# One layer of a fused two-block kernel: the 64-step scan with heads on their own partition halves and one triangle of its inverse

## What is computed

```python
    def step(state, inp):
        r_t, k_t, v_t, w_t, kk_t, a_t = inp
        sa = jnp.einsum('bhij,bhj->bhi', state, -kk_t)
        state = (state * w_t[:, :, None, :]
                 + sa[..., None] * (kk_t * a_t)[:, :, None, :]
                 + v_t[..., None] * k_t[:, :, None, :])
        y_t = jnp.einsum('bhij,bhj->bhi', state, r_t)
        return state, y_t
    ...
    _, y = lax.scan(step, state0, (seq_first(r_h), seq_first(k_h), seq_first(v_h),
                                   seq_first(w_h), seq_first(kk_h), seq_first(a_h)))
    y = jnp.moveaxis(y, 0, 1)
    mean = jnp.mean(y, axis=-1, keepdims=True)
    var = jnp.mean(jnp.square(y - mean), axis=-1, keepdims=True)
    y = ((y - mean) * lax.rsqrt(var + GN_EPS)).reshape(B, S, RWKV_CH) * gn_w.astype(F32) + gn_b.astype(F32)
    ...
    y = y + bonus.reshape(B, S, RWKV_CH)
    return (y * g.astype(F32)).astype(p_rwkv.dtype)
```

## Time and profile before

| | us |
|---|---|
| median of three runs (1587.70, 1587.82, 1590.32) | 1587.82 |
| time of the profiled execution | 1589.53 |
| its span, first to last instruction | 1587.7 |
| PE busy in it | 1328.5 |
| DVE busy in it | 1034.8 |

### The profile page before, as it was taken

How to read it: one execution, slowest core, us unless ns; L and a number is a source line. 1 busy time by engine, 2 the same in 40 slices (tenths; PEclk the granted TensorE clock), 3 DMA queues, 4 the chain that set the end, 5 groups by cost and what they waited for, 6 DMA issues and landing times. The chain is left out here.

```text
span 1587.7 us, 18244 instructions
## 1 busy us (share of the span) xinstructions
PE 1328.5 (84%) x6818; PEld 917.9 (58%) x6818; DVE 1034.8 (65%) x2387; ACT 405.7 (26%) x843; POOL 295.3 (19%) x297
## 2 busy tenths in 40 slices
PE   5996788998568888888888877777999788799988
PEld 2974377777533333333333322224899667799978
DVE  1697377775677878787787777655552677455442
ACT  3314300003501111111110101012553444544431
POOL 0003200000054444444344334330000000000000
PEclk9997799899889999999999999999999898899999
DMA  9455821117299999999999999997355006245443
GB/s 399 176 193 231 339 110 73 62 64 308 80 396 421 422 420 421 421 422 421 420 412 415 420 421 407 421 421 300 111 208 209 4 1 266 106 160 194 178 159 133
DMA packets 48184, 426.59 MB, mean 269 GB/s; under 512 B 5344, under 2 KB 5472, under 8 KB 5600
## 3 DMA queue, kind: packets, MB, share of 16 engines
q0 software_dynamic: 36864, 268.45, 40.8%
q1 hardware_dynamic: 11232, 156.98, 25.6%
HBM read 424.36 MB, written 1.05 MB: 268 GB/s over the span
## 5 line engine op out<-in xcount | busy, mean ns | idle before, releaser
L1277 PE MATMUL bank<-arena 128*128 128x512 f32 x1024 | 499.5, 615 | 128.9 <-DVE arena L1420 128.6
L1277 PEld LDWEIGHTS bank<-arena 128*128 128x128 f32 x1024 | 176.5, 190 | 436.9 <-DVE arena L1420 285.3
L1458 DVE CUSTOM_DVE_ANT_0 arena<-arena 128x1024 f32<-128x1024 f32 x256 | 313.6, 1225 | 149.2 <-DMA arena<-experts_in,arena 146.0
L1204 POOL DMA_INDIRECT arena<-experts_in,arena x256 | 274.5, 1072 | 606.0 <-PE bank L1277 352.9
L467 PE MATMUL bank<-rounded,rounded 128*128 128x256 f32 x1144 | 334.9, 293 | 45.7 <-DVE rounded L430 36.0
L469 PE MATMUL bank<-rounded,ring_r 128*128 128x256 f32 x1144 | 328.4, 287 | 0.0
L468 PE MATMUL bank<-rounded,rounded 128*128 128x256 f32 x1144 | 327.2, 286 | 0.0
L444 DVE TENSOR_TENSOR ring_r<-ring,rounded 128x1024 fp32r<-128x1024 f32 (+2 forms) x137 | 171.9, 1268 | 144.1 <-ACT rounded L439 144.1
L467 PEld LDWEIGHTS bank<-rounded,rounded 128*128 128x128 f32 x1144 | 222.5, 194 | 50.4 <-issue 27.6
L468 PEld LDWEIGHTS bank<-rounded,rounded 128*128 128x128 f32 x1144 | 223.7, 196 | 3.0 <-issue 2.9
L469 PEld LDWEIGHTS bank<-rounded,ring_r 128*128 128x128 f32 x1144 | 223.3, 195 | 0.0
(11 more groups left out here) (264 smaller groups left out, 1109.8 us busy)
## 6 DMA issues: line engine op xcount, KB each, us to landing
...
arena<-experts_in,arena POOLq DMA_INDIRECT x256, 13.6
...
```

The source lines that it names most:

```text
L1204: pool.indirect_dma_start(rows[:, r % GRING, :], None, experts_in, bass.IndirectOffsetOnAxis(ap=expert[:, tt, at:at + 1], axis=0)).then_in ...
L1277: ins = pe.matmul(psum[2 * tt + half][:, :], diag[:, r % DIAGS, :], rows[:, r % GRING, D + 512 * half:D + 512 * half + 512], start=(h == 0 ...
L1458: dve.tensor_tensor_reduce(rows[:, r % GRING, 0:D], rows[:, r % GRING, 0:D], utok[:, tt, :], 1.0, 0.0, ALU.mult, ALU.add, hdot[:, r:r + 1] ...
```

## The change

**Operands.** The block-diagonal operands and all their memsets and copies are gone, in the preparation and in the scan. Each head's product is a matmul of its own of 64 by 64 on its own partitions (`product`, two for each tile, first head 0, then head 1, into the same bank at partitions 0 to 63 and 64 to 127).

**Steps.** A step covers all four tiles in one bank. Only one triangle of the inverse is kept (R, with the powers P and M). The inverse of the whole triangle isn't made: V1 applies the diagonal part's inverse to the values, and H1, H2, H3 apply x = V1 - S x three times. There are 12 steps of `INVERSE`, which don't need the state, and 7 of `STATE`.

**Order.** `ORDER` runs the inverses of chunks 0 and 1 side by side, then the state steps of chunk 0 between the inverse steps of chunk 2, those of chunk 1 between those of chunk 3, and then the state steps of chunks 2 and 3 alone. Rows 13 to 17 and their columns are put between steps. ACT copies the results of eight of the steps, DVE the rest. The statistics of each chunk are taken one part at a time behind later steps, and the root of the variance by two functions, Ln and Exp, once for each chunk (`roots_of`). The scaling and the bias of the normalization are folded into `gate` and `bv`.

```diff
         B0 = 8960
-        BDk, BDb, BDc, BDr, BDv = (area(B0 + i * 2048, CT, NC, 2, C) for i in range(5))
-        RH = area(B0 + 10240, CT, NC, 2, C)
...
-                for b in (BDk, BDb, BDc, BDr, BDv):
-                    g(pool.memset(b[0:64, :, :, 1, :], 0.0))
-                    g(pool.memset(b[64:128, :, :, 0, :], 0.0))
                 pool.memset(dec[:, :, :, 0:1], 1.0).then_inc(rw["zero"], 1)
-                pool.wait_ge(rw["xs"], NPROJ)
-                for hh in range(2):
-                    s = slice(64 * hh, 64 * hh + 64)
-                    g(pool.tensor_copy(BDv[s, :, :, hh, :], by_chunk(xs[s, 8:12, :])))
 
             @block.vector
...
-                v(dve.tensor_tensor(T0, T0, T3, ALU.mult))
-                for hh in range(2):
-                    s = slice(64 * hh, 64 * hh + 64)
-                    dve.tensor_copy(BDk[s, :, :, hh, :], by_chunk(T0[s]))
...
-                act.wait_ge(rw["kap"], CT)
-                act.wait_ge(rw["rs"], CT)
-                act.wait_ge(rw["bs"], 1)
-                for hh in range(2):
-                    s = slice(64 * hh, 64 * hh + 64)
-                    act.copy(BDc[s, :, :, hh, :], RH[s, :, :, 0, :])
-                    act.copy(BDr[s, :, :, hh, :], RH[s, :, :, 1, :])
-                    act.copy(BDb[s, :, :, hh, :], bS[s])
                 for q in (9, 10, 11):
                     act_mod_row(act, q)
...
+        INVERSE = ("G1", "G3", "G2", "PM2", "TVB", "L1R", "PM4", "TK", "L2R", "M8", "L3R", "SM")
+        STATE = ("RN", "V1", "H1", "H2", "H3", "ST", "Y")
+        ORDER = [(k, c) for k in INVERSE for c in (0, 1)]
+        for c in (0, 1):
+            ORDER += [("G1", c + 2), ("RN", c), ("G3", c + 2), ("G2", c + 2), ("V1", c), ("PM2", c + 2), ("TVB", c + 2),
+                      ("H1", c), ("L1R", c + 2), ("PM4", c + 2), ("H2", c), ("TK", c + 2), ("L2R", c + 2), ("M8", c + 2),
+                      ("H3", c), ("L3R", c + 2), ("ST", c), ("SM", c + 2), ("Y", c)]
+        ORDER += [(k, 2) for k in STATE] + [(k, 3) for k in STATE if k != "ST"]
...
+                for k, c in ORDER:
+                    n = MADE[k, c]
+                    if n >= SBANKS:
+                        ok, oc = ORDER[n - SBANKS]
+                        if ok in BY_DVE:
+                            from_dve(pe, READ_LAST[ok], oc)
+                        else:
+                            from_act(pe, ok, oc)
...
+                    def product(terms, width=C, at=0):
+
+                        for ct in range(CT):
+                            for i, (l, r_) in enumerate(terms):
+                                for s in HEAD:
+                                    ins = pe.matmul(bank[s, at + ct * width:at + (ct + 1) * width], l(ct)[s], r_(ct)[s],
                                                     start=(i == 0), stop=(i == len(terms) - 1))
...
+                    elif k == "L1R":
+                        from_act(pe, "PM2", c)
+                        from_dve(pe, "R0", c)
+                        ins = product([(m_, of(R[c]))])
+                    elif k == "PM4":
+                        product([(m_, p_)])
+                        ins = product([(p_, m_)], at=CT * C)
...
+                    elif k == "SM":
+                        from_dve(pe, "R3", c)
+                        ins = product([(of(OT[c]), of(R[c]))])
+                    elif k == "RN":
+                        from_act(pe, "TVB", c)
+                        from_dve(pe, "N", c)
+                        terms = [(of(N[c]), vs)]
+                        if c:
+                            from_dve(pe, "Ss", c - 1)
+                            terms.append((kap, of(Ss[c % 2])))
+                        ins = product(terms)
+                    elif k == "V1":
+                        from_dve(pe, "Rn", c)
+                        from_dve(pe, "R3", c)
+                        ins = product([(of(R[c]), of(Rn))])
+                    elif k == "H1":
+                        from_act(pe, "V1", c)
+                        from_act(pe, "SM", c)
+                        ins = product([(of(Sm[c]), of(V1))])
+                    elif k == "H2":
+                        from_dve(pe, "X1", c)
+                        ins = product([(of(Sm[c]), of(X))])
+                    elif k == "H3":
...
+                    elif k == "H3":
+                        from_dve(pe, "X2", c)
+                        ins = product([(of(Sm[c]), of(X))])
+                    elif k == "ST":
+                        from_dve(pe, "U", c)
+                        from_act(pe, "TK", c)
+                        ins = product([(of(tk[c]), vs), (tb, of(Us[c % 2]))])
+                    else:
+                        from_dve(pe, "U", c)
+                        from_dve(pe, "RK", c)
+                        terms = [(of(RK[c]), vs), (of(RB[c]), of(Us[c % 2]))]
+                        if c:
+                            terms.append((rd, of(Ss[c % 2])))
+                        ins = product(terms)
+                    ins.then_inc(rc_mm, 1)
...
+                    elif (k, c) == ("SM", 1):
+                        pe_mod_row(pe, 13)
...
+                    elif (k, c) == ("RN", 2):
+                        pe_mod_row(pe, 15)
+                    elif (k, c) == ("H1", 2):
+                        pe_mod_cols(pe, 15)
+                    elif (k, c) == ("H3", 2):
+                        pe_mod_row(pe, 16)
+                    elif (k, c) == ("RN", 3):
+                        pe_mod_cols(pe, 16)
+                    elif (k, c) == ("H1", 3):
+                        pe_mod_row(pe, 17)
+                    elif (k, c) == ("Y", 3):
+                        pe_mod_cols(pe, 17)
                 pe_mod_row(pe, 18)
                 pe_mod_row(pe, 19)
...
+                pe.wait_ge(rc_y, NC)
+                pe.wait_ge(rc_ev, len(dve_count))
+                pe.wait_ge(rc_copy, len(act_count))
+                for ct in range(CT):
+                    for c in range(NC):
+                        for s in HEAD:
+                            ins = pe.matmul(psum[ct // 2][s, (ct % 2) * T + c * C:(ct % 2) * T + (c + 1) * C], yn[s, c, ct, :],
...
+                def statistics(c, part):
+
+                    mu, vr = st[:, 0, c], st[:, 1, c]
+                    wide = [P, CT, C]
+                    if part == 0:
+                        from_act(dve, "Y", c)
+                        v(dve.tensor_reduce(mu, yn[:, c], AX_X, ALU.add))
+                        v(dve.tensor_scalar(mu, mu, 1.0 / C, None, ALU.mult))
+                    elif part == 1:
+                        v(dve.tensor_tensor(yn[:, c], yn[:, c], mu.unsqueeze(2).to_broadcast(wide), ALU.subtract))
+                    elif part == 2:
+                        v(dve.tensor_tensor(sq, yn[:, c], yn[:, c], ALU.mult))
+                    elif part == 3:
+                        dve.tensor_reduce(vr, sq, AX_X, ALU.add).then_inc(rc_var, 1)
+                    else:
+                        dve.wait_ge(rc_sd, 2 * c + 2)
+                        dve.tensor_tensor(yn[:, c], yn[:, c], st[:, 2, c].unsqueeze(2).to_broadcast(wide),
+                                          ALU.mult).then_inc(rc_y, 1)
...
+                    if k == "G1":
+                        ticked(dve.tensor_tensor(PM[c][:, 0], pairs[:, :, 0, :], mask("dS"), ALU.mult))
+                        ticked(dve.tensor_tensor(RB[c], pairs[:, :, 1, :], mask("mI"), ALU.mult))
+                        from_dve(dve, "P", c)
+                        ticked(dve.tensor_tensor(R[c], mask("eye"), PM[c][:, 0], ALU.subtract))
+                    elif k == "G3":
+                        ticked(dve.tensor_tensor(PM[c][:, 1], ps, mask("dL"), ALU.mult))
...
+                        ticked(dve.tensor_tensor(Us[c % 2] if k == "H3" else X, V1, ps, ALU.subtract))
+                    else:
+                        new, decay = Ss[(c + 1) % 2], dec[:, :, c, C:C + 1].to_broadcast([P, CT, C])
+                        if c:
+                            v(dve.tensor_tensor(new, Ss[c % 2], ps, ALU.add))
+                            ticked(dve.tensor_tensor(new, new, decay, ALU.mult))
+                        else:
...
+                    elif k in ("RN", "H1", "H2", "H3") and c >= 2:
+                        part = ("RN", "H1", "H2", "H3").index(k)
+                        statistics(c - 1, part)
+                        if k == "H3":
+                            statistics(c - 1, 4)
+                for part in range(5):
+                    statistics(NC - 1, part)
...
+                def roots_of(c):
+                    act.wait_ge(rc_var, c + 1)
+                    act.activation(st[:, 2, c], st[:, 1, c], ACT.Ln, bias=epsc[:, 2:3], scale=1.0 / C).then_inc(rc_sd, 1)
+                    act.wait_ge(rc_sd, 2 * c + 1)
+                    act.activation(st[:, 2, c], st[:, 2, c], ACT.Exp, scale=-0.5).then_inc(rc_sd, 1)
...
+                        ins = act.copy({"TK": tk[c], "M8": PM[c][:, 1], "SM": Sm[c], "V1": V1, "Y": yn[:, c]}[k], tiles4(bank))
```

(14 more changed lines are left out.)

391 lines of the change are left out of this document (151 added, 240 removed).

## The result

The changed kernel takes **1514.38 us** (median of 4 runs, 1513.95 to 1516.71) against 1587.86 (1587.7 to 1590.32): ratio 0.954, 95% interval 0.9525 to 0.9554. Forecast were 1518, in a range of 1498 to 1560. Measured again beside other kernels later it took 1517.55 (5 runs), ratio 0.9558, interval 0.9545 to 0.9571. The profiled execution has a span of 1512.5 us.

The account below looks back on a forecast made before the run. PE bounds the block, DVE next. Block parts sum to 109.0 us, plus 7 for half clock: 116 against 184.5; with 1.7 from the preparation, 70 less: 1587.8 - 70 = 1518, range 1498 to 1560.

Parts of the forecast that it names:

- inverses 0 and 1: Block, inverses of the first two chunks: 208 slots at 0.065, 32 at 0.112, rows, columns and gaps, 20.4 us.
- inverse 2, state 0: Block, chunk 2's inverse with chunk 0's state: 120 + 72 slots, trips hidden behind the other chain, 16.5 us.
- inverse 3, state 1: Block, chunk 3's inverse with chunk 1's state: 120 + 88 slots, 0.9 waiting for ACT's root of chunk 0, 16.2 us.
- state 2 with its wait: Block, chunk 2's state alone: 12.1 us with open trips, then 5.1 waiting for DVE's scaling behind ACT's root; 17.2.
- state 3: Block, chunk 3's state alone: 9.8 us at full clock, 4.0 more for half clock.
- behind it: Block after the last state: roots, statistics, scaling, transposes, then rows and columns, 25.6 us, about 3 more at half clock.
- preparation: Before the block: without six ACT copies columns 9 come sooner, 1.7 us less (0 to 2.6); DVE and POOL copies delay nobody.
- Price of a slot: PE in the block: one head 0 record with its head 1 partner, side by side, 0.065 us (floor 0.058, roof 0.12).
- Rival 1: Partners take turns (same bank or one weight path): block sum 151 us, kernel 1553; chance 0.24 shared with a mixed clock.
- Rival 2: Array counts as idle and stays at 1.2 GHz: block sum 174 us, kernel 1576; chance 0.05.
- rival 3: Slower: partners in turn and half clock together, rows and slots 156 us more, block sum 265, kernel 1667; chance 0.03.
- Rival 4: Waits, not PE, set the first stages: open trips of 0.7 add 20 us, 1538; partly included in the forecast's 0.60.

Follow-up runs that it names:

- e1: The changed kernel with each step's products reordered, all four tiles of head 0, then all four of head 1: 1531.57 us.
- e6: e7 with the chunks one after the other, each chunk's inverse steps and then its state steps: 1521.81 us.
- e7: The changed kernel with roots taken for two chunks at a time and all scaling by DVE behind the last state step: 1505.21 us.
- e5: The changed kernel with eight spare products, their results overwritten, issued by PE in the wait before state 3: 1510.14 us.
- e3: The changed kernel with ACT's six preparation copies put back, onto an area that nobody reads: 1514.58 us.
- e9: The changed kernel with POOL's ten memsets and two copies and ACT's six copies put back, onto an area nobody reads: 1518.78 us.
- e11: e7 with SP holding back the slot loads for rows 16 and 17 until later steps are made: 1504.16 us.
- e2: The changed kernel with POOL's ten memsets and two copies of the preparation put back, onto an area that nobody reads: 1518.1 us.

## Why the prediction was right, point by point

| part of the block | computed | measured in after |
|---|---|---|
| head | 3.3 | 3.3 |
| inverses 0 and 1 | 20.4 | 23.7 |
| inverse 2, state 0 | 16.5 | 15.0 |
| inverse 3, state 1 | 16.2 | 17.5 |
| state 2 with its wait | 17.2 | 17.1 |
| state 3 | 9.8 + 4.0 | 13.9 |
| behind it | 25.6 + 3 | 28.5 |
| block | 116 | 119.0 |
| preparation | 47.0 | 41.8 |

The spans of the two profiles differ by 75.2 us: 65.4 in the block, 6.9 in the preparation, 2.0 ahead of it and 1.0 behind, where no edit is. The forecast's 70 stand for the first two, so it was 2.2 off there. Of the 65.4 the runs show 16.4 for the partners (e1) and 16.1 for the overlap of two chains (e6, on e7), and the head gave 7.5. The rest, some 25 by this estimate, is left for the shorter inverse and the steps of one bank; no run takes these apart.

- **Price of a slot.** 0.065 computed, 0.064 to 0.067 measured with the last record's length in it, 0.058 from pair to pair: the floor of the prediction, for the partner starts 0.003 behind and its 0.007 for that weren't needed. 0.117 when partners are taken apart (e1). The reading that set it, pairs at half clock with loads that overlap and loads that start 0.01 apart, was the right neighbour.
- **Rival 1, partners in turn.** It falls. The Trainium skill (TensorEngine Tiling (Array Packing), Restrictions and Gotchas) forbids different row tiles the same PSUM bank at the same time; here partners lie on different rows and on different partitions of one bank, and 40 slots ran in 2.55 us. That the rule holds for row tiles which share their partitions no run here shows.
- **Rival 2, half clock throughout.** It falls: 1.00 in the two middle parts, and 0.91 in the first, where PE stood. In rival 3, slower, the terms for slots and rows add up to 152 and not 156; nothing hangs on it.
- **Rival 4, waits set the first stages.** PE idles 0.25 and 1.2 us in the two parts with a state beside an inverse. (Y of chunk 0 comes behind row 14 and so behind the mark between them: by steps the two parts are 16.1 and 16.4, for 16.5 and 16.2 computed.) e6 shows what the interleaving is worth, 16 us.
- **State 2 and 3.** The named wait came at its place, 4.94 for 5.1, with the named releasers, and the half clock behind it at the named size; e5 takes each away.
- **Inverses 0 and 1: 3.3 too few.** The step left out was PE's own instructions. Half the work per record, twice the records in a time: a load of 16 KB lasts 3.4 us where PE is dense, and 19 to 24 in the chunks of the kernel before, and the prediction costed DMA for slots alone ("so DMA isn't later than PE"). The stand is 2.0, and the half clock behind it makes most of another 2.0: ACT's copy of SM of chunk 1 comes at 25.3 us of the block, in e3, e9 and e11, without the stand, at 21.3. Without both the part would take 19.7, so the other terms were 0.7 too many.
- **Preparation: 5.2 too many.** The step that failed is "The DVE and POOL copies that go had no one waiting". POOL's writes slowed DVE beside them, and DVE's chain leads over ACT and columns 7 to row 8 (3.4, e2). For ACT's copies the wait of columns 9 was right, but row 11 went from half clock to full as well (3.36 us before, 1.92 after): 3.4 for 1.7 (e3).
- These two misses have opposite signs, and part of one is the cause of the other: without ACT's copies the slots reach further into the block, over PE's dense run. So the total came nearer to the forecast than its terms did: errors of 5.2 and 3.3 cancel in part, and that is luck.
